# Mixture-of-experts decoder layer: expert loop over 64 experts, overflow rows in units of 32 through a second loop

## The chip, the cores and the metric

One core of one Trainium2 chip. The metric is the device time of one launch of the whole layer in microseconds (us), median of several runs. Beside it stands one profiled execution with its own span, from its first to its last instruction.

## The reference

One layer for 1104 tokens (16 meta tokens, a prompt of 1024, 8 samples of 8 tokens): latent attention and a gated linear recurrence side by side, a merge, a layer norm, and then the part that this change touches, a mixture of experts:

```python
scores = sigmoid(x @ router_w)                       # x: (N, 1024), 64 experts
_, idx = top_k(scores + router_bias, 8)              # 8 experts for each token
gate = scores[idx] / sum(scores[idx]) * 2.5
y[token] += gate * (silu(x @ w_gate[e]) * (x @ w_up[e])) @ w_down[e]   # 1024 -> 256 -> 1024, all e in idx
out = layer_norm(ALPHA * x + y + shared_expert(x))
```

All arrays are float32. The tokens choose their experts by data: 1104 x 8 = 8832 rows over 64 experts, 138 on average. Evaluating the routing of the reference on its own inputs gives more than 160 rows for 5 experts (162, 166, 168, 171 and 183 rows), and no expert has more than 192.

## The kernel before, in words

The layer runs in stages, each a block in which the five engines run their own programs and wait on semaphores. The last three matter here.

**`stage_route`** (L1895) computes the first layer norm, the router scores and the shared expert. For each (token, expert) pair it writes an entry (token number, factor) to a slot of a table in DRAM (`slot_table`, scattered by GpSimd at L1990). The slot is `place * 64 + expert`, where `place` is the row's position among the rows of its expert. Then VectorE counts on how many experts lie above 160 rows: `over` (L2256 to L2259), five chained steps for further multiples of 160, a running sum `ob`, and from it a list of blocks (`cols`, turned by TensorE at L2109 into `blocks_i`) and the number of pairs of blocks (`pairs_i`). SyncE (SP) loads the table back to SBUF (L1977, L1979) as `ent_main` (rows 0 to 127 of each block) and `ent_rest` (rows 128 to 159, four times below each other), for all seven layers of 160 rows. The main output rows `y` of shared expert and residual go to DRAM as `y_rows`.

**`stage_experts`** (L2339) is a loop over pairs of blocks. A block is 160 slots of one expert: 128 rows of `xg` ("main") and 32 rows of `xg_rest` ("rest"). Blocks 0 to 63 are the first 160 rows of the 64 experts, and further blocks hold what an expert has above 160 rows, again as full blocks of 160 slots whose empty slots carry an index out of range, which the indirect transfers skip. An odd number of blocks is filled up with an empty one. The two blocks of a pair use the buffers s = 0 (`mla` in the profile for gate and up) and s = 1 (`mix`).

For each block SP loads 3 x 1 MB of weights (`weights`, L2396): gate and up once the rest products of the same buffer are done (`rest_full`), down once the copy of the previous block's output is done (`part_copied`). GpSimd (POOL) copies the indices (`pick`), gathers the rows from `x_rows` (`gather`, L2435) and adds the results to `y_rows` by an indirect accumulating transfer (`scatter`, L2452), main and rest each; before the next scatter it waits until the last one has landed (`y_out`, seen as a wait of L2426). TensorE turns the rows (`turn` L2498, `turn_rest` L2503), multiplies the main rows in three products of split weights (high part, low part, `PRODUCTS`, L2529 and L2550) and the rest rows with the unsplit weights (L2519 and L2563). ScalarE makes the high parts (`round_weights`, L2601), VectorE the low parts (`part_weights`, L2676). The engines work on different blocks at once: while block n is multiplied down, block n + 1 goes through gate and up and block n + 2 is turned.

Which expert a block belongs to and which layer of the table it reads is data, so SP reads registers from SBUF at the head of each pair (`expert`, L2394, three loads) and POOL too (`layer`, L2422, five loads). Each engine reads the number of pairs at its start (L2365).

**`stage_out`** (L2750) loads `y_rows` back, when the last scatter has landed and the block has been closed, and computes the second layer norm.

## Time and profile before

| | |
|---|---|
| runs (median of 3) | 2381.16 us (2374.51 to 2383.53) |
| the profiled execution's own time | 2375.11 us |
| its span | 2373.3 us |
| TensorE / VectorE / ScalarE / GpSimd busy | 2167.6 / 1413.6 / 1092.8 / 872.3 us |
| mean granted TensorE clock | 0.957 of full |
| stage of the experts | about 1345 to 2328 us of the span |
| blocks of 160 slots | 70 (140 scatters of L2452, two for each) |

Busy time counts an engine's instructions. The share of DMA is the mean busy share of the core's 16 DMA engines. Idle time before an instruction is put down to what ended it.
### The profile page before, as it was taken

The numbers are of one execution on the slowest core, as the hardware profiler recorded it, in microseconds if no ns is written. First come the engines' busy times: TensorE is split into PE (matmuls) and PEld (weight loads), VectorE is DVE, ScalarE is ACT, GpSimd is POOL, SyncE is SP. The second block draws the span as 40 slices with busy tenths as digits, with TensorE's granted clock in tenths as the row PEclk, the third lists the DMA queues.
The fourth block names the chain that finished last, engine by engine and source line by source line (L and its number), as shares of the span: only waits on it lengthen the run. The fifth ranks groups of instructions, "written<-read, shape, count | busy, mean of one in ns | idle before, by whom it ended". The sixth has DMA issues, their size and how long they took to land. (4 is left out here: it accounts for less than half of the span.)

```text
span 2373.3 us, 47274 instructions
## 1 busy us (share of the span) xinstructions
PE 2167.6 (91%) x17792; PEld 1695.0 (71%) x17792; DVE 1413.6 (60%) x2572; ACT 1092.8 (46%) x1700; POOL 872.3 (37%) x957
## 2 busy tenths in 40 slices
PE   7999899899867799999999899999999999999990
PEld 7666667679856799996555477777777777777760
DVE  4667455422186545544672467777777777777765
ACT  3355433322143333331220266676666666676652
POOL 0112311000142000000343257767776767677763
PEclk9999899899978899999999999999999999999995
DMA  4000333311000555441042489999999999999944
GB/s 154 14 1 1 135 118 134 103 54 45 31 25 2 192 176 177 148 131 60 28 153 96 156 280 319 303 309 323 304 298 318 313 308 327 302 310 314 290 148 169
DMA packets 104577, 419.42 MB, mean 177 GB/s; under 512 B 26278, under 2 KB 37606, under 8 KB 74502
## 3 DMA queue, kind: packets, MB, share of 16 engines
q1 hardware_dynamic: 64038, 320.69, 37.9%
q0 software_dynamic: 40144, 96.21, 15.7%
q8 instruction: 74, 1.21, 0.2%
q10 hardware_dynamic: 288, 1.05, 0.1%
q14 instruction: 33, 0.27, 0.0%
HBM read 374.69 MB, written 63.09 MB: 184 GB/s over the span
## 5 line engine op out<-in xcount | busy, mean ns | idle before, releaser
L2676 DVE TENSOR_TENSOR split<-mix,split 128x2048 fp32r<-128x2048 f32 x140 | 320.1, 2287 | 241.2 <-ACT split L2601 203.1
L2452 POOL DMA_INDIRECT y_rows<-mix x140 | 363.5, 2596 | 117.2 <-issue 86.9
L2529 PE MATMUL banks<-split 128*128 128x512 f32 x1680 | 402.7, 395 | 0.3 <-DVE split L2676 0.3
L2529 PEld LDWEIGHTS banks<-split 128*128 128x128 f32 x1680 | 310.4, 188 | 77.0 <-issue 14.4
L2601 ACT CAST split<-mix 128x2048 fp32r<-128x2048 f32 x140 | 266.9, 1908 | 0.0
L1990 POOL DMA_INDIRECT slot_table<-route x72 | 69.5, 966 | 465.8 <-DVE route L2228 446.2
L2550 PE MATMUL banks<-split 128*128 128x512 f32 x840 | 211.4, 401 | 4.7 <-DVE split L2705 4.7
L1777 PE MATMUL banks<-merge_split 128*128 128x368 f32 x1152 | 201.6, 332 | 4.5 <-DVE merge_split L1842 4.5
L1777 PEld LDWEIGHTS banks<-merge_split 128*128 128x128 f32 x1152 | 195.5, 190 | 5.1 <-DVE merge_split L1842 5.0
L2435 POOL DMA_INDIRECT hq<-x_rows,mix x136 | 149.7, 1100 | 82.9 <-POOL mix L2427 60.1
L2550 PEld LDWEIGHTS banks<-split 128*128 128x128 f32 x840 | 153.8, 190 | 34.9 <-issue 4.8
L2676 DVE TENSOR_TENSOR split<-mla,split 128x2048 fp32r<-128x2048 f32 x70 | 159.6, 2280 | 7.5 <-ACT split L2601 7.5
L2426 POOL COPY mix<-mix 128x2 int32 x138 | 111.9, 811 | 123.1 <-DMA y_rows<-mix 99.8
L2623 ACT COPY mix<-banks 128x512 f32<-128x512 f32 x140 | 82.3, 588 | 116.0 <-PE banks L2550 115.2
L2601 ACT CAST split<-mla 128x2048 fp32r<-128x2048 f32 x70 | 134.1, 1916 | 0.0
L1764 PE MATMUL banks<-merge_split 128*128 128x368 f32 x576 | 105.7, 334 | 8.2 <-DVE merge_split L1842 4.6
L1828 ACT ACTIVATE merge_rest<-banks 128x368 f32<-128x368 f32 x48 | 23.0, 478 | 189.6 <-PE banks L1777 189.6
L1109 PE MATMUL banks<-inputs_split 128*128 128x512 f32 (+1 forms) x432 | 103.5, 401 | 5.7 <-DVE inputs_split L1183 5.6
L1764 PEld LDWEIGHTS banks<-merge_split 128*128 128x128 f32 x576 | 98.8, 191 | 9.0 <-DVE merge_split L1846 4.8
L1109 PEld LDWEIGHTS banks<-inputs_split 128*128 128x128 f32 (+1 forms) x432 | 80.6, 187 | 28.4 <-DVE inputs_split L1183 7.5
L2498 PE MATMUL banks<-base,hq 128*128 128x128 f32 x560 | 85.2, 275 | 14.0 <-DMA hq<-x_rows,mix 9.7
L1125 PE MATMUL banks<-inputs_split 128*128 128x368 f32 x576 | 96.8, 330 | 0.0
(401 smaller groups left out, 4023.5 us busy)
## 6 DMA issues: line engine op xcount, KB each, us to landing
mix<-in_w_exp_down SPq DMA_DIRECT2D x70, 1024.0 KB
mla<-in_w_exp_gate SPq DMA_DIRECT2D x35, 1024.0 KB
mla<-in_w_exp_up SPq DMA_DIRECT2D x35, 1024.0 KB
mix<-in_w_exp_gate SPq DMA_DIRECT2D x35, 1024.0 KB
mix<-in_w_exp_up SPq DMA_DIRECT2D x35, 1024.0 KB
raw<-in_w_merge SPq DMA_DIRECT2D x32, 768.0 KB
merge_rest<-in_w_merge SPq DMA_DIRECT2D x15, 768.0 KB
raw<-in_w_cols SPq DMA_DIRECT2D x11, 512.0 KB, 4.6
```

The source lines that it names most:

```text
L1109: ins = pe.matmul(PS[0:rows(i), 4 + u % 4], x[a][:, k, 128 * i:128 * i + rows(i)], w[:, p % 4, b, 512 * (k % 2):512 * (k % 2 + 1)], start= ...
L1125: ins = pe.matmul(bank3(g)[:, n], cols[:, a, k], x[b][:, k, CH * n:CH * (n + 1)], start=(k == 0 and j == 0), stop=(k == KD - 1 and j == 2))
L1764: ins = pe.matmul(branch_bank(u), w[u % WR][:, a, GATE + 128 * k:GATE + 128 * (k + 1)], b[:, e, c, k], start=(k == 0 and t == 0), stop=(k ...
L1777: ins = pe.matmul(gate_bank(u), w[u % WR][:, a, 128 * k:128 * (k + 1)], x[:, c, k], start=(k == 0 and t == 0), stop=(k == KD - 1 and t == 2))
L2426: pool.tensor_copy(dst[:, s, 0:2].bitcast(I32), ent_main[:, bass.ds(at, 1)].rearrange("p a w -> p (a w)").bitcast(I32)).then_inc(sem, 1)
L2435: pool.indirect_dma_start(out=dst[:, s], out_offset=None, in_=src, in_offset=bass.IndirectOffsetOnAxis(ap=gi[:, s, 2 * hf:2 * hf + 1].bitc ...
L2452: pool.indirect_dma_start(out=dst, in_=src[:, s], in_offset=None, compute_op=ALU.add, out_offset=bass.IndirectOffsetOnAxis(ap=si[:, s, 2 * ...
L2498: ins = pe.transpose(PS[:, XBANK[r], 128 * j:128 * (j + 1)], xg[:, s, 128 * k:128 * (k + 1)], S.ident)
L2529: ins = pe.matmul(PS[:, MBANK].rearrange("p (j n) -> p j n", j=2), xr[:, a, k], wr[:, s, GATE:UP + 1, b, DEXP * k:DEXP * (k + 1)], start=( ...
L2550: ins = pe.matmul(PS[:, DBANK[c]], hr[:, a, f], wdr[:, b, at:at + 512], start=(f == 0 and j == 0), stop=(f == 1 and j == 2))
L2601: act.copy(parts(s, j)[:, HI], raw[s][j]).then_inc(rounded[j], 1)
L2676: dve.tensor_tensor(parts(s, j)[:, LO], raw[s][j], parts(s, j)[:, HI].bitcast(F32), ALU.subtract).then_inc(parted[j], 1)
```

## The change

The loop of pairs runs over the 64 experts alone, with constant bounds: 31 passes and a last pair that is written out. SP and POOL no longer load registers in it, since expert and entry number follow from the loop counter. The rows that an expert has above 160 are cut into units of 32 (`MINIS`, at most 256), and a second loop over pairs of units, of at least one pass, stands behind the first on every engine. A unit uses the unsplit weights alone, as the rest rows do.

In `stage_route` the chain over `over` has 29 steps in place of 5 (`LAYERS` = 30), the columns of the list are worked out for two times 128 units, TensorE turns four columns in place of two, and only the first 160 rows of each expert are loaded back from the table.

In the second loop SP reads expert e and layer j of a unit from SBUF, waits for a free entry buffer (`mini_free`), loads the 32 entries four times, and then 3 x 1 MB of weights. POOL raises `mini_free` by two only once the last scatter of block 63 has landed, and by one after each unit's scatter has landed. POOL gathers the rows of both units of a pair, then scatters the first, waits for it to land, scatters the second, and waits again.

```diff
-VCAP = -(-T // CAP) * CAP
-KOVER = VCAP // CAP - 1
-SLOTS = EXPERTS * VCAP
-LAYERS = VCAP // CAP
+LAYERS = -(-(T - CAP) // REST)
+SLOTS = EXPERTS * (CAP + REST * (LAYERS + 1))
+MINIS = 256
...
-        for k in range(1, KOVER):
-            own.link(dve.scalar_tensor_tensor(over[:, k], PS[:, 6, 0:EXPERTS], float(CAP * (k + 1)), over[:, k - 1], ALU.is_gt, ALU.add))
+        for k in range(1, LAYERS):
+            own.link(dve.scalar_tensor_tensor(over[:, k % 2], PS[:, 6, 0:EXPERTS], float(CAP + REST * k), over[:, (k - 1) % 2], ALU.is_gt, ALU.add))
...
+        for z in range(2):
+            m = pid[:, z:z + 1]
+            (seven small steps that give expert and layer of 128 units)
...
     @block.sync
-        last = last_pair(sp)
-        with sp.Fori(0, last) as it:
-            e = [expert(2 * it + 1 + s) for s in range(3)]
+        with sp.Fori(0, LASTP) as it:
             for s in range(2):
                 n = 2 * it + s
                 sp.wait_ge(rest_full, n + 1)
-                weights(s, GATE, e[s + 1])
-                weights(s, UP, e[s + 1])
+                weights(s, GATE, n + 2)
+                weights(s, UP, n + 2)
                 sp.wait_ge(part_copied, 3 * n + 3)
-                weights(1 - s, DOWN, e[s])
+                weights(1 - s, DOWN, n + 1)
+        pairs = mini_pairs(sp)
+        with sp.Fori(0, pairs) as it:
+            for s in range(2):
+                m = 2 * it + s
+                e = sp.value_load(X.blocks_i[0:1, 0, bass.ds(m, 1)], min_val=0, max_val=EXPERTS - 1)
+                j = sp.value_load(X.blocks_i[0:1, 1, bass.ds(m, 1)], min_val=0, max_val=LAYERS)
+                sp.wait_ge(mini_free, m + 1)
+                for q in range(4):
+                    src = overflow[bass.ds(j, 1), bass.ds(e, 1)].rearrange("j e r w -> (j e r) w")
+                    sp.dma_start(ent_mini[REST * q:REST * (q + 1), s].bitcast(I32), src).then_inc(mini_in[s], 16)
+                sp.wait_ge(rest_full, EXPERTS - 1 + m)
+                weights(s, GATE, e)
+                weights(s, UP, e)
+                sp.wait_ge(mini_copied, m + 1)
+                weights(s, DOWN, e)
...
     @block.gpsimd
-            at = [layer(2 * it + j) for j in range(2 + (2 if not ends else 0) + (gathers == 2))]
+        pool.wait_ge(y_out[1], 32 * (LASTP + 1))
+        pool.sem_inc(mini_free, 2)
+        with pool.Fori(0, pairs) as it:
+            for s in range(2):
+                pool.wait_ge(mini_index, 4 * (2 * it + s) + 4)
+                pool.wait_ge(xrest_full, EXPERTS - 1 + 2 * it + s)
+                (gather of xg_rest[:, s]).then_inc(mini_x[s], 16)
+            for s in range(2):
+                pool.wait_ge(mini_copied, 2 * it + s + 3)
+                (scatter of y_rest[:, s]).then_inc(mini_out[s], 16)
+                pool.wait_ge(mini_out[s], 16 * (it + 1))
+                pool.sem_inc(mini_free, 1)
...
     @block.tensor
+        def mini(s, it):
+            m = 2 * it + s
+            pe.wait_ge(mini_x[s], 16 * (it + 1))
+            pe.wait_ge(mini_copied, m + 2)
+            turn_rest(s, None)
+            pe.wait_ge(xrest_copied, EXPERTS + 1 + m)
+            for j in (GATE, UP):
+                pe.wait_ge(raw_in[j][s], 16 * (EXPERTS // 2 + it + 1))
+            rest_products(s)
+            pe.wait_ge(h_made, 2 * EXPERTS + 1 + m)
+            pe.transpose(PS[:, HBANK, 2 * MAIN:3 * MAIN], h_rest, S.ident).then_inc(hT_full, 1)
+            pe.wait_ge(hr_parted, EXPERTS + 1 + m)
+            pe.wait_ge(raw_in[DOWN][s], 16 * (EXPERTS // 2 + it + 1))
+            down_rest_products(s).then_inc(mini_full, 1)
...
     @block.scalar
+                act.wait_ge(rest_full, EXPERTS + 1 + m)
+                gate_rest()
+                act.wait_ge(mini_free, m + 1)
+                act.wait_ge(mini_full, m + 1)
+                act.copy(y_rest[:, s], PS[:, EBANK, 0:256]).then_inc(mini_copied, 1)
...
     @block.vector
+        with dve.Fori(0, pairs) as it:
+            for s in range(2):
+                dve.wait_ge(mini_in[s], 64 * (it + 1))
+                (four steps that turn the 32 entries into indices of quarter rows; mini_index + 1 each)
+            for s in range(2):
+                (copy of the turned rows, product with the sigmoid, product with factor and up, copy of hT_rest)
```

The lines in parentheses stand for several lines of code. `rest_products` and `down_rest_products` are the loops of L2515 to L2520 and L2560 to L2564 under names of their own, and `gate_rest` is L2609 and L2610.

## Rows read from the trace of the kernel before

**Rows 1.** Stretches of the expert loop: width, busy of each engine, PEclk, DMA share, GB/s.
```profile
1400.00:2227.00 827.00, 806.90 (x7785) 619.40 (x7783) 609.29 (x728) 556.03 (x725) 575.71 (x605) 1.00 0.97 312
2213.00:2290.00 77.00, 76.14 (x751) 59.16 (x748) 57.10 (x67) 53.58 (x69) 58.03 (x60) 1.00 0.76 247
```
**Rows 2.** The page, part 5: all scatters of the expert loop.
```profile
L2452 POOL DMA_INDIRECT y_rows<-mix x140 | 363.5, 2596 | 117.2 <-issue 86.9
```
**Rows 3.** Timeline of SP's queue: issues of the down weights, one for each block.
```profile
1379.66 0.33 SPq L2399 DMA_DIRECT2D mix<-in_w_exp_down  x1
...
2213.77 0.33 SPq L2399 DMA_DIRECT2D mix<-in_w_exp_down  x1
...
2281.22 13.45 SPq L2399 DMA_DIRECT2D mix<-in_w_exp_down  x2
```
**Rows 4.** What TensorE waited for, 1379 to 2295 us: total, times, longest.
```profile
PE banks L2498 <- DMA hq<-x_rows,mix: 9.7, 11, 1.6
```
**Rows 5.** Timeline of the loop's first block, TensorE just resumed: start, duration.
```profile
1345.67 0.63 PE L2503 MATMUL banks<-base,hq 128*128 128x128 f32 x2
...
1349.29 0.42 DVE L2684 COPY mix<-banks 128x256 f32<-128x256 f32 x1
...
1349.77 3.16 PE L2519 MATMUL banks<-mla,mix 128*32 128x128 f32 x64 [2.61 <-DVE mix L2684]
...
1352.98 0.27 ACT L2609 ACTIVATE mix<-banks 64x128 f32<-64x128 f32 x1 [3.16 <-PE banks L2519]
...
1353.95 0.34 DVE L2693 SCALAR_TENSOR_TENSOR mix<-mix 64x128 f32<-64x128 f32 x1
```
**Rows 6.** Timeline of the loop's end.
```profile
2281.26 1.95 PE L2519 MATMUL banks<-mla,mix 128*32 128x128 f32 x64
...
2313.53 0.19 POOL L2426 COPY mix<-mix 128x2 int32 x1 [1.43 <-DMA y_rows<-mix]
...
2315.91 1.07 PE L2563 MATMUL banks<-mix 128*32 128x256 f32 x16
...
2317.05 0.37 ACT L2628 COPY mix<-banks 128x256 f32<-128x256 f32 x1 [0.44 <-PE banks L2563]
2318.26 1.56 POOL L2452 DMA_INDIRECT y_rows<-mix  x1 [4.43 <-ACT mix L2628]
```
**Rows 7.** Stretches around TensorE's pauses, columns as in the first group.
```profile
1349.00:1351.00 2.00, 1.24 (x24) 1.16 (x28) 2.00 (x5) 0.82 (x1) 1.13 (x3) 0.50 0.03 8
1353.00:1356.00 3.00, 2.75 (x12) 2.30 (x13) 1.37 (x4) 2.99 (x4) 0.98 (x1) 1.00 0.46 171
2312.00:2314.00 2.00, 2.00 (x6) 1.63 (x5) 0.00 (x0) 0.00 (x0) 0.41 (x3) 0.50 0.04 1
```
**Rows 8.** The page, part 6: one small transfer, median us from issue to landing.
```profile
out<-out SPq DMA_DIRECT2D x1, 64.0 KB, 2.1
```
**Rows 9.** A stretch in which little but weights is loaded, in the stage before.
```profile
1246.00:1250.00 4.00, 3.54 (x38) 2.80 (x38) 2.69 (x21) 0.43 (x1) 3.09 (x4) 1.00 1.00 410
```
**Rows 10.** Timeline: a gather inside the loop and TensorE's wait for it.
```profile
1597.79 1.04 POOL L2435 DMA_INDIRECT hq<-x_rows,mix  x1 [0.30 <-issue]
...
1606.90 0.65 PE L2498 MATMUL banks<-base,hq 128*128 128x128 f32 x4 [1.38 <-DMA hq<-x_rows,mix]
```
**Rows 11.** Transfers that write or read `y_rows`: us from issue to landing.
```profile
DMA to landing us min/median/max: 2.6/4.1/12.7
```
**Rows 12.** Register loads by line: min/median/max ns, first and last start us.
```profile
L2422 POOLq TENSOR_LOAD <-base x5: 287/290/292, 1616.1 to 1618.6; - x5
```
**Rows 13.** Timeline of the list of blocks in the stage before.
```profile
1281.94 1.26 DVE L2258 SCALAR_TENSOR_TENSOR route<-banks,route 128x64 f32<-128x64 f32 x5
...
1284.99 0.15 DVE L2270 TENSOR_SCALAR route<-route 128x1 f32<-128x1 f32 x1
...
1292.78 0.38 PE L2109 MATMUL banks<-base,route 128*1 128x128 f32 x2
```
**Rows 14.** DMA queues, 1400 to 2290 us: packets of the instruction queue, MB, share.
```profile
q14 instruction: 1, 0.01, 0.0%
```

More of the change, by code:

```diff
@@ L2466, in body @@
                     pool.sem_inc(passed, 1)
-                    gather(*ahead(s, it, 3), at[s + 3])
-                scatter(s, it, at[s], first)
+                    gather(*ahead(s, it, 3), n + 3)
+                scatter(s, it, n, first)
         for j in range(3):
```

203 lines of the change are left out of this document (118 added, 85 removed).

## The prediction

> **What bounds the kernel now.** I read three views, in this order. The stretches of the expert loop come first [rows 1]: in 827 us TensorE is busy for 806.9 at the full clock, and the 16 DMA engines are busy for 97% at 312 GB/s, so the loop sits at two limits at once. In the stretch that holds the blocks above 64, whose indirect transfers move almost nothing, the DMA share falls to 0.76 and TensorE stays at 99%. Second, the timeline of SP's queue gives the period [rows 3]. There is one down issue for each block. From 1379.66 to 2213.77 they are 61 blocks, 13.67 us each. The last one starts at 2294.33 (2281.22 + 13.45 - 0.34), six blocks after 2213.77: 80.6 us, 13.4 each. So a block costs 13.4 us on TensorE alone and 0.3 more when the transfers are full. Third, the waits: of TensorE's 20.1 us of idle time in those 827 us, the only large transfer wait is for gathered rows, 9.7 us in 11 waits over the whole loop [rows 4].
>
> There are 140 scatters, two for each block, so 70 blocks ran [rows 2]: 64 experts, the 5 blocks above 160 rows that the reference's routing gives, and one empty block to make pairs. All five experts stay at or under 192 rows, so the new loop gets 5 units and one empty one, three passes. What is bought for six blocks is six units.
>
> **Removed: six blocks.** 80.6 us [rows 3]. They are taken out of a saturated loop, so this counts in full.
>
> **Added: a chain that nothing covers.** The second loop starts on POOL's word, once the last scatter of block 63 has landed. SP stands at `mini_free` before it, and behind that wait stand the entries and all the unit's weights, so nothing is prefetched during the last blocks. I price one unit, from its rows landed to its output copied (C): two turns 0.63, copy 0.42, rest products 3.16, two steps on ScalarE at 0.27 and two on VectorE at 0.34, one turn of h at half of 0.63, a copy of 0.22 (half of 0.42), 16 down products, an output copy of 0.37 [rows 5, 6]. TensorE's clock decides. The figures of rows 5 were taken at 1.2 GHz, the level granted after a pause [rows 7]; at 2.4 GHz the same 64 products take 1.95 and the 16 take 1.07 [rows 6]. I scale 1.07 by 3.16 / 1.95 to 1.7 for 1.2 GHz, and the turns by the same ratio down for 2.4. With eight handovers of about 0.07 (1352.93 to 1352.98, 2316.98 to 2317.05) [rows 5, 6], C is 8.6 at 1.2 GHz and 6.4 at 2.4 GHz.
>
> After C comes the scatter (D): 0.84 from ScalarE's copy to its start, 1.56 for itself, 1.43 until the next instruction of POOL is let go [rows 6], 3.9 with a little for rows that are not skipped. Before C comes the gather (G): the same 0.84, 1.04 for itself [rows 10], and a landing that the trace does not show alone. Its bounds are 1.43, the landing of an almost empty scatter [rows 6], and 8.07, from the end of a gather at 1598.83 to TensorE at 1606.90 under full DMA load [rows 10]. The small stored transfer takes 2.1 [rows 8]. The DMA engines are mostly free in the second loop, so I take 2.0, and G is 3.9.
>
> The order of the programs makes a pass serial. POOL gathers for the next pair only when this pair's second scatter has landed, and TensorE turns the second unit only when the first one is copied. The first scatter runs beside the second unit's chain and costs nothing (3.9 under a chain of 6.4 or more). The next pair's first weights are asked for when that first scatter lands, and they need 3.15 MB / 410 GB/s = 7.7 us plus 2.1 [rows 8, 9]; they hide under the rest of the second unit, the scatter and the gather. VectorE makes the indices of both units before it copies the first one's rows: SP's four issues (0.33 each and a little between them, 0.45), a landing of 2.1 and four steps of 0.15 [rows 3, 8, 13] end about 4.5 us after the second scatter landed, as G and the turn do (3.9 + 0.63). I add 0.5 for the tie. A later pass is thus 3.9 + 0.5 + 2C + 3.9.
>
> The first pass starts with its entries: 1.9 of issues, 2.1 to land, 0.6 for indices, G, about 8.5 us. But the second unit's entries stand in SP's queue behind the first unit's 3 MB, so VectorE's copy may wait until about 12.6 (2.8 of issues + 2.1 + 7.7). The bounds are 8.5 plus a turn and 12.6, and I take the later. The Trainium skill, "DMA: Bandwidth & Descriptors", section "Queues, rings and completion order", says that one queue's descriptors are consumed in ring order on each DMA engine; no row here shows it, and by the opposite the sum would be 3.5 us smaller.
>
> With all at 1.2 GHz the first pass is 12.6 + 8.0 + 8.6 + 3.9 = 33.1 (the first turn lies inside 12.6) and a later one 25.5: 84.1 in all. With all at 2.4 GHz it is 12.6 + 6.0 + 6.4 + 3.9 = 28.9 and 21.1: 71.1. Which level holds? TensorE idles for more than 7 us before each first unit (D and G), and after a pause at the loop's end it stood at 0.50 at 2312; after it resumed at 1349.77 the clock was back at 1.00 in the stretch from 1353 [rows 7]. So the first unit of a pass runs at 1.2 GHz, and the second one probably in part at 2.4. I give the second one the middle, 1.1 less each: 84.1 - 3.3 = **80.8 us**.
>
> **Changed in the loop.** POOL's five register loads for each pair lie between two scatters and the next gather, five at 0.29 with the steps between them, 1616.1 to 1618.9 [rows 12]. Without them some gathers go out up to about 1 us sooner. The most that can be won is the 9.7 us of rows 4, and nothing if the DMA engines, at 97%, only serve the same bytes in another order. I take 3. SP's three loads lie ahead of a wait for the rest products and cost nothing now; POOL's wait for the landing of a scatter comes later than they did, too. The last scatter before the second loop is now of a real block: the median landing of all is 4.1 from issue against 1.56 + 1.43 [rows 6, 11], **+1.1**. The engines' load of the number of pairs moves from the head of the stage, where all wait for it, to behind the loop, where it hides under the last scatter: -0.7, two and a half times a load of 0.29 [rows 12].
>
> **Changed in the stage before.** Five chained steps take 1.26 us, so 24 more take 6.05, and the second half of the columns some 1.4 (scan and columns together took the 1.9 from 1283.20 to 1285.14). The list was ready at 1285.14 and is now at about 1292.6; TensorE comes for it at 1292.78, after its shared products [rows 13]. So it is covered by a hair, and each microsecond above that would show in full. TensorE turns four columns and not two: +0.4. The smaller table load ends under the same shared products and wins nothing.
>
> **The sum.** -80.6 + 80.8 + 1.1 - 0.7 + 0.4 - 3.0 = -2.0. The profiled execution took 2375.1 by its own time (span 2373.3), the median of the runs is 2381.2, 6.1 more. I forecast 2373.1 for a profiled run and **2379 us** for the median. By half a percent, 11.9 us, a measurement of this kernel can tell a change from none.
>
> **Rivals.**
> *The clock holds and the loop speeds up.* TensorE stays at 2.4 GHz through the second loop, and the earlier gathers win the whole 9.7: -80.6 + 71.1 + 1.1 - 0.7 + 0.4 - 9.7 = -18.4, 2363 us. For it: bursts of a pass follow each other closely, 1.00 came back within about 3 us [rows 7]. Against: the pause between passes, and 97% DMA share. Chance 0.20.
>
> *Slower: the unit's indirect transfers stand behind weights.* While the gather goes out, 3 MB of weights may still be moving, and then it lands after 8.07 as in rows 10, not 2.0. The first pass has its copy at 8.5 + 6.1 instead of 12.6, 2.0 more; each later one costs 6.1 more, so the second loop takes 95.0 and the sum is +12.2: 2393 us. It decides when a later pass loses about 6 us. With all at 1.2 GHz and no gain in the loop as well, it comes to 2400. For it: weights and rows share the engines. Against: by my times the weights have landed when the later gathers start. Chance 0.14.
>
> *The jumps cost.* Each engine jumps back twice in the second loop, and the instructions may have to be fetched again on the path. By the nearest row, a transfer's 2.1 us [rows 8] for each of the entry and two jumps, this is +6: 2385 us. The first loop argues against it: over 30 jumps of every engine in 890 us, and the instruction queue moved one packet [rows 14]. The Trainium skill, "Runtime: NRT & Kernel Launch", section "Instruction fetch mechanics", says that a taken branch to outside the window of instructions held forces a fetch before execution goes on; the trace bears this out only in so far as these loops seem to fit. Chance 0.08.
>
> *It doesn't do what it says.* An expert above 192 rows would bring a unit more, two of them a pass more, +25 us. The routing gives none, and 70 blocks agree. I give it no share.
>
> **How the numbers follow.** The likeliest case has 0.58, its own range 2370 to 2391. The range for all reaches from the first rival's 2363 to 2398, between the second rival's 2393 and the 2400 that it gives with the other costs at their upper ends. Faster by over 0.5% (under 2369.3): 0.20, the first rival. Slower (over 2393.1): 0.14, the second. Within: 0.66.
>
> **What the profile after would show.** The down issues should stop after 64 blocks with the period near 13.6, and 128 large-loop scatters. The second loop should last 71 to 95 us from the last landing, its first pass longer than the two others by 7 to 8. TensorE should be busy for under half of it, DMA in bursts near 400 GB/s, the clock between 0.5 and 1. L2109's four turns should still start at about 1292.8. I would be wrong if gathers or entries landed much later than 2.1 us, if the weights of a unit were on the path, or if the first loop's period moved by more than 0.15 us, since that is multiplied by 62.

## The result, and the profile after

The changed kernel takes 2390.76 us (median of 7 runs, 2385.66 to 2395.09), the kernel before 2380.02 us on the same chip (7 runs). The ratio is 1.0061, 95% interval 1.0043 to 1.008: slower by 0.6%, or 10.7 us, where I had forecast 2379 and no change that can be told. The time lies in my range, but the sign is that of a case to which I had given 0.14. The profiled execution has a span of 2388.9 us; that of before had 2373.3.

The page of the changed kernel, tenths of 40 equal slices of the span (59.7 us each):

```profile
PE   8999899899877799999999799999999999999430
...
PEclk9999899899978899999999999999999999999755
DMA  4000423311100655431141489999999999999554
```

The two slices before the last show what is new: TensorE falls from nine tenths to four and three at a clock of 0.7 and 0.5, while the DMA engines are half idle. Most of these two slices is the second loop. First the part that answers to [rows 1] and [rows 3], the windows of the first loop (length, then busy us of each engine with its instructions, granted clock, DMA share, GB/s) and the end of SP's queue in it (start, length, what was issued):

```profile
1400.00:2190.00 790.00, 776.71 (x7497) 596.64 (x7490) 583.99 (x697) 535.89 (x698) 559.95 (x581) 1.00 0.97 314
```

```profile
1384.74 0.33 SPq L2403 DMA_DIRECT2D mix<-in_w_exp_down  x1
...
2212.90 0.34 SPq L2403 DMA_DIRECT2D mix<-in_w_exp_down  x1
```

From block 2 to block 63 it is (2212.90 - 1384.74) / 61 = 13.58 us a block, against 13.67 in [rows 3]: 5.9 us less over the loop. TensorE's wait for gathered rows is 3.8 us in 7 waits, against 9.7 in 11 [rows 4].

Now the second loop, the timeline from the last main scatter (L2465) on. L2428 loads a unit's entries, L2817 makes indices of them, L2403 loads its weights, L2500 gathers, L2531 turns the rows, L2539 and L2589 are the products, L2736 copies the output, L2506 scatters; in brackets is the idle time ahead and what ended it:

```profile
2238.24 1.55 POOL L2465 DMA_INDIRECT y_rows<-mix  x1 [0.30 <-issue]
2243.02 1.74 SPq L2428 DMA_DIRECT2D mix<-slot_table  x4
...
2248.01 1.79 SPq L2428 DMA_DIRECT2D mix<-slot_table  x4
...
2253.79 0.69 PE L2531 MATMUL banks<-base,hq 128*128 128x128 f32 x2 [18.71 <-DMA hq<-x_rows,mix]
2255.96 0.67 DVE L2817 TENSOR_SCALAR mix<-mix 32x1 int32<-32x1 int32 x4 [9.38 <-DMA mix<-slot_table]
...
2265.11 1.64 POOL L2506 DMA_INDIRECT y_rows<-mix  x1 [6.49 <-ACT mix L2736]
...
2269.88 1.73 SPq L2428 DMA_DIRECT2D mix<-slot_table  x4
2270.67 0.37 ACT L2736 COPY mix<-banks 128x256 f32<-128x256 f32 x1 [2.59 <-PE banks L2589]
2271.86 0.35 SPq L2403 DMA_DIRECT2D mla<-in_w_exp_gate  x1
2271.91 1.57 POOL L2506 DMA_INDIRECT y_rows<-mix  x1 [5.16 <-ACT mix L2736]
2272.30 0.38 SPq L2403 DMA_DIRECT2D mla<-in_w_exp_up  x1
...
2281.19 1.72 SPq L2428 DMA_DIRECT2D mix<-slot_table  x4
2282.27 1.07 POOL L2500 DMA_INDIRECT hq<-x_rows,mix  x1 [8.79 <-issue]
...
2286.18 3.83 PE L2539 MATMUL banks<-mla,mix 128*32 128x128 f32 x64 [0.70 <-DVE mix L2821]
...
2292.15 1.94 PE L2589 MATMUL banks<-mix 128*32 128x256 f32 x16 [0.32 <-DVE mix L2827]
...
2303.69 0.37 ACT L2736 COPY mix<-banks 128x256 f32<-128x256 f32 x1 [3.60 <-PE banks L2589]
...
2311.86 1.72 SPq L2428 DMA_DIRECT2D mix<-slot_table  x4
...
2335.79 1.58 POOL L2506 DMA_INDIRECT y_rows<-mix  x1 [7.84 <-ACT mix L2736]
```

From the end of the last main scatter (2239.79) to the end of the last unit's (2337.37) it is **97.6 us**, where my terms make 81.9 (80.8, and 1.1 for the landing of the real block). This stretch is what I call the length of the second loop. The rows from 2271.91 on show the largest part. The second unit's scatter ends at 2273.48, and SP is let go by its landing only at 2281.19, 7.7 us later; POOL stands idle for 8.79 us before its next gather. As that scatter began, SP asked for 3 MB of weights for the next pass (from 2271.86 on). The windows of that landing, of the second pass's, and of the three passes:

```profile
2273.50:2281.20 7.70, 0.00 (x0) 0.00 (x0) 0.00 (x0) 0.00 (x0) 0.00 (x0) 0.52 0.97 391
2304.90:2311.80 6.90, 0.00 (x0) 0.00 (x0) 0.00 (x0) 0.00 (x0) 1.58 (x1) 0.50 0.84 320
```

```profile
2243.00:2281.20 38.20, 9.21 (x166) 6.39 (x166) 4.29 (x20) 1.81 (x6) 5.33 (x4) 0.68 0.66 250
2281.20:2311.90 30.70, 13.67 (x166) 8.45 (x166) 3.71 (x16) 1.81 (x6) 5.32 (x4) 0.50 0.57 214
2311.90:2338.00 26.10, 12.51 (x166) 8.15 (x166) 3.12 (x12) 1.81 (x6) 5.32 (x4) 0.57 0.33 123
```

While the scatter lands, no engine works and the transfers run at 391 GB/s: those are the weights, 3.15 MB in about 8 us. The first two passes take 38.2 and 30.7 us, where I had 33.1 and 25.5 for the low clock. And the clock was low for both units of the second pass, not for the first alone.

The first theory after the result was therefore: contention of each pass's last scatter with the next pass's weights costs 10 of the 15.7 us that were missed, the low clock 4 to 5. The rivals: the clock alone; the jumps; the loop's first start.

### The profile page after: what moved, and what is told of

Read it like the earlier page. It is cut to its first block and busy times, and to the rows that moved or that the text cites. A ratio compares the mean times of both kernels' runs of the same rounds, so it can differ in the third digit from the quotient of the medians.

```text
span 2388.9 us, 45337 instructions
## 1 busy us (share of the span) xinstructions
PE 2125.3 (89%) x17518; PEld 1659.3 (69%) x17518; DVE 1370.1 (57%) x2580; ACT 1043.0 (44%) x1648; POOL 832.3 (35%) x908
## 5 line engine op out<-in xcount | busy, mean ns | idle before, releaser
L2743 DVE TENSOR_TENSOR split<-mix,split 128x2048 fp32r<-128x2048 f32 x128 | 292.6, 2287 | 220.2 <-ACT split L2655 188.6
L2465 POOL DMA_INDIRECT y_rows<-mix x128 | 333.2, 2603 | 101.3 <-issue 75.6
L2560 PE MATMUL banks<-split 128*128 128x512 f32 x1536 | 367.8, 395 | 0.0
L2560 PEld LDWEIGHTS banks<-split 128*128 128x128 f32 x1536 | 283.4, 188 | 69.9 <-issue 12.7
L2655 ACT CAST split<-mix 128x2048 fp32r<-128x2048 f32 x128 | 243.9, 1907 | 0.0
L2581 PE MATMUL banks<-split 128*128 128x512 f32 x768 | 193.2, 401 | 4.6 <-DVE split L2743 4.6
L2448 POOL DMA_INDIRECT hq<-x_rows,mix x124 | 137.7, 1110 | 75.4 <-POOL mix L2440 54.5
L2581 PEld LDWEIGHTS banks<-split 128*128 128x128 f32 x768 | 140.8, 190 | 32.1 <-DVE split L2743 4.8
L2439 POOL COPY mix<-mix 128x2 int32 (+1 forms) x126 | 113.2, 899 | 111.8 <-DMA y_rows<-mix 90.1
L2743 DVE TENSOR_TENSOR split<-mla,split 128x2048 fp32r<-128x2048 f32 x64 | 146.0, 2281 | 4.2 <-ACT split L2655 4.2
L2655 ACT CAST split<-mla 128x2048 fp32r<-128x2048 f32 x64 | 122.6, 1916 | 0.0
L1123 PE MATMUL banks<-inputs_split 128*128 128x368 f32 x576 | 96.8, 330 | 0.0
L1123 PEld LDWEIGHTS banks<-inputs_split 128*128 128x128 f32 x576 | 96.7, 188 | 0.1
```

What stands on the lines that cost most here:

```text
L1123: ins = pe.matmul(bank3(g)[:, n], cols[:, a, k], x[b][:, k, CH * n:CH * (n + 1)], start=(k == 0 and j == 0), stop=(k == KD - 1 and j == 2))
L2439: pool.tensor_copy(dst[:, s, 0:2].bitcast(I32), ent_main[:, bass.ds(at, 1)].rearrange("p a w -> p (a w)").bitcast(I32)).then_inc(sem, 1)
L2448: pool.indirect_dma_start(out=dst[:, s], out_offset=None, in_=src, in_offset=bass.IndirectOffsetOnAxis(ap=gi[:, s, 2 * hf:2 * hf + 1].bitc ...
L2465: pool.indirect_dma_start(out=dst, in_=src[:, s], in_offset=None, compute_op=ALU.add, out_offset=bass.IndirectOffsetOnAxis(ap=si[:, s, 2 * ...
L2560: ins = pe.matmul(PS[:, MBANK].rearrange("p (j n) -> p j n", j=2), xr[:, a, k], wr[:, s, GATE:UP + 1, b, DEXP * k:DEXP * (k + 1)], start=( ...
L2581: ins = pe.matmul(PS[:, DBANK[c]], hr[:, a, f], wdr[:, b, at:at + 512], start=(f == 0 and j == 0), stop=(f == 1 and j == 2))
```

## The experiments

The runs of this part were made in three groups, each on one chip of its own, each with the kernel before beside them: the first four kernels with it at 2359.93 us, the unaltered kernel, register loads, early start and interleaved order at 2362.63, the 64 fillers and the last kernel at 2360.16. Between groups I compare each kernel's distance to the kernel before, and stretches within traces.

### No second loop

```diff
-        pairs = mini_pairs(...)
-        with ...Fori(0, pairs) as it:      # on all five engines
-            ...
```

> The changed kernel without its second loop on any engine; POOL still waits for the last scatter of block 63. It leaves out the rows above 160 of five experts. The changed kernel's trace has 97.6 us from the end of block 63's last scatter (2239.8) to the end of the last unit's scatter (2337.4). If the second loop is what made the kernel slower than forecast, this one takes 95 to 98 us less than the changed kernel (2390.8), 2293 to 2296. If instead the earlier stages or the first loop got slower by the change, the difference stays what I had forecast for the loop, about 82 us, and this kernel takes about 2309.

Measured: 2279.47 us (one run), span 2277.7, 80.5 below the kernel before. The expected 2293 to 2296 was worked out at the first comparison's level, where the kernel before takes 20 us more, so only the distance can be used. The unaltered changed kernel was run in the next group and stands 18.4 above it, so its second loop costs about 98.9 us. The same number tests all the rest of my sum: without the added loop it says -80.6 + 1.1 - 0.7 + 0.4 - 3.0 = -82.8, and -80.5 was measured. Everything but the 80.8 came out right together, within 2.3. That is closer than one run can show, since the ten runs of the kernel before in this group lie from 2355.91 to 2366.26, and it tests the sum and none of its terms.

### Weights of 64 columns in place of 2048

```diff
+        def thin(s, j, e):
+            sp.dma_start(raw[s][j][:, 0:64], src[:, 0:64]).then_inc(raw_in[j][s], 16)
...
-                weights(s, GATE, e)
+                thin(s, GATE, e)          # the same for UP and DOWN
```

> The changed kernel, where the second loop loads only 64 of 2048 columns of each weight block of a unit, with all semaphores and orders as they are. It leaves out most of the weights of the units, so their rows are wrong. Theory A, the second scatter of a pass lands late (7.6 and 5.3 us after its issue ends, against 3.1 and 1.8 for the first scatter) because it shares the DMA engines with the 3 MB that the first scatter's landing let go: then both land within 2 to 3 us, and the first pass starts its copy at about 9 us instead of 13.7 after the second loop's first entry load. Second loop 97.6 - 8 - 4.5 = about 85 us. Theory B, a scatter of 128 quarter rows with an accumulate simply takes that long behind a second scatter, whatever else moves: the landings stay at 5 to 8 us, and only the first pass is shorter, about 93.

Measured: 2366.91 us (one run). From the last main scatter's end to the last unit's scatter's end it is 81.3 us (2232.24 to 2313.55). The ends of its first two passes, and the windows of its three:

```profile
2261.79 1.57 POOL L2511 DMA_INDIRECT y_rows<-mix  x1 [6.38 <-ACT mix L2741]
...
2265.78 1.73 SPq L2433 DMA_DIRECT2D mix<-slot_table  x4
...
2285.22 1.58 POOL L2511 DMA_INDIRECT y_rows<-mix  x1 [4.89 <-ACT mix L2741]
...
2289.24 1.72 SPq L2433 DMA_DIRECT2D mix<-slot_table  x4
```

```profile
2235.40:2265.80 30.40, 12.01 (x166) 7.80 (x166) 4.28 (x20) 1.81 (x6) 5.32 (x4) 0.61 0.09 16
2265.80:2289.30 23.50, 9.30 (x166) 6.48 (x166) 3.70 (x16) 1.81 (x6) 5.31 (x4) 0.72 0.10 17
2289.30:2314.00 24.70, 12.36 (x166) 8.15 (x166) 3.13 (x12) 1.81 (x6) 5.31 (x4) 0.57 0.04 7
```

The scatter now lands 2.4 us after its end, twice (2263.36 to 2265.78, 2286.80 to 2289.24), where it took 7.7 and 5.3 beside the weights. So what the weights' transfers cost is real, and the theory that the scatters are slow by themselves (93 us expected) is out. The clock stayed low too (0.61, 0.72, 0.57, against 0.68, 0.50, 0.57 in the changed kernel), but not everywhere: the second unit of the second pass ran at the full clock (6.5 us from scatter to scatter). Added up, the six chains are 49.8 us here and 51.7 in the changed kernel, so 2.0 of the 16.3 us that the loop is shorter are the clock's, and the clock alone cannot be what was missed. The later passes, 23.5 and 24.7, now lie between my 21.1 and 25.5: a later pass with its weights gone takes what I had predicted with them. (The whole, 81.3 against my 81.9, agrees more closely than it should: my first pass had the wait of the entries behind weights in it, which is gone here.)

### Weights asked for first

```diff
         with sp.Fori(0, pairs) as it:
             for s in range(2):
-                (entries of unit s, weights of unit s)
+                unit_weights(s, 2 * it + s)
+            for s in range(2):
+                unit_entries(s, 2 * it + s)
```

> The changed kernel with one order turned round on SP: in a pass the weights of both units are asked for first (gate and up once the rest products of the buffer are done, down once the last output is copied), then the entries of both, which wait for their buffer. Same bytes, same products. Theory A: the first pass no longer waits for entries behind 3 MB (copy at 9 us, not 13.7), and gate and up of the next pass have landed before the second scatter; only 1 MB of down still meets it. Second loop 97.6 - 4.5 - 6 = about 87, the kernel about 2380, 0.5% faster than the changed one, close to the kernel before. Theory B (scatters slow by themselves): 93, the kernel 2386.

Measured: 2373.64 us (7 runs, 2365.49 to 2383.41), ratio to before 1.0067 [1.0043, 1.0091], 13.7 us above it where the unaltered changed kernel stands 18.4 above. The second loop takes 88.0 us. The first pass gained most: 17.9 us from the first entries to the first scatter, against 22.5 in the unaltered kernel's run of the next group. The later passes gained little, 30.2 and 28.5 us from first scatter to first scatter against 30.6 and 30.7. SP's queue shows why:

```profile
2254.27 0.33 SPq L2403 DMA_DIRECT2D mix<-in_w_exp_down  x1
2255.11 1.57 POOL L2514 DMA_INDIRECT y_rows<-mix  x1 [6.24 <-ACT mix L2744]
2256.10 8.66 SPq L2435 DMA_DIRECT2D mix<-slot_table  x8
...
2265.42 1.07 POOL L2508 DMA_INDIRECT hq<-x_rows,mix  x1 [8.74 <-DVE mix L2825]
```

Both units' weights are now asked for from 2242 to 2254, while the units are still at work, and the small transfers behind them are late in the same way, with the DMA engines at a share of 0.98 or more until 2260: eight entry loads take 8.66 us where the first eight of the loop took 4.95, and POOL waits 8.74 us for the indices. The wait changed its name, not its length. That the whole came near the expected 87 is partly luck: against the unaltered kernel's 98.1 us the first pass gives 4.6, the later passes together 2.5 where 6 were expected, and 3.0 come from the last unit, which ran at the full clock (6.5 us from scatter to scatter against 9.5).

### Filler products ahead of each pass, 40 and 64

```diff
         def mini(s, it):
+            if s == 0:
+                for _ in range(40):       # 64 in the second kernel
+                    pe.matmul(PS[:, MBANK]..., xr[:, HI, 0], wr[:, 0, GATE:UP + 1, HI, 0:DEXP], start=True, stop=True)
             pe.wait_ge(mini_x[s], 16 * (it + 1))
```

> The changed kernel with 40 more products of 128x512 into an unused bank on TensorE ahead of each pass's wait for gathered rows, about 10 us of work in time in which TensorE idles. In the changed kernel a unit's chain from its turn to its output's copy takes 9.8 and 9.5 us in the second pass, all at a granted clock of 0.50, and 6.8 for the second unit of the first pass, at 1.00. Theory clock: all chains fall to about 6.8, the second loop to 97.6 - 3 - 5.7 - 4.5 = about 84 us. If the chain's length is in the handovers and not in the clock, it stays within 2 us of 97.6. If the added products run past the landing of the rows, the passes get longer by that.

Measured with 40: 2369.86 us (one run), but the second loop took 96.8 us, not 84. Its windows around the second pass, three microseconds each (the clock is third from the end, then DMA share and GB/s):

```profile
2257.00:2260.00 3.00, 3.00 (x15) 2.49 (x14) 0.00 (x0) 0.00 (x0) 0.00 (x0) 1.00 0.99 388
2260.00:2263.00 3.00, 0.78 (x4) 0.32 (x2) 0.00 (x0) 0.00 (x0) 0.10 (x1) 1.00 0.09 26
2263.00:2266.00 3.00, 0.00 (x0) 0.00 (x0) 0.58 (x4) 0.00 (x0) 0.97 (x1) 0.84 0.36 72
2266.00:2269.00 3.00, 1.92 (x26) 1.55 (x30) 0.42 (x1) 0.00 (x0) 1.03 (x1) 0.50 1.03 431
```

The clock is full while the filler runs, and back at 0.50 when the unit's own products start at 2266.4. So 40 were too few to test the price. The run stands 9.9 us above the kernel before, where the unaltered kernel stands 18.4 above. Its second loop gives only 1.3 of the difference, and 3.2 lie ahead of it (the last main scatter ends at 2219.39, in the unaltered kernel's profile on another chip at 2222.57); one run does not tell more.

> The changed kernel with 64 filler products, not 40, ahead of each pass of units; their sums are never read. 40 of them took 9.0 us and ended 5.6 us before the second pass's rows landed; the granted clock was 1.00 while they ran and 0.50 again when the unit's own products began, and the second loop took 96.8 us against 98.1 in the unaltered kernel on this chip. 64 should take 14.8 us and end as the rows land (14.9 us after the previous chain's end). If the low clock costs what the prediction took (2.2 us a unit) or the 2.6 that chains of 9.5 and 6.8 us differ by, the four units of passes two and three give back 9 to 10: a second loop of 87 to 89 and a kernel of about 2371 where the unaltered one takes 2381. If only loads, gathers and landings matter there, since the products wait for them anyway, it stays at 95 to 98 and 2378 to 2383. If the filler itself outlasts the landing, the loop becomes longer.

Measured with 64: 2376.96 us (7 runs), ratio 1.0067 [1.0043, 1.0091] to before, second loop 95.0 us. In the second pass the clock now held through both units, in the third pass through the first unit, and the loop still gained only 3 us. The timeline of the second pass:

```profile
2277.00 1.96 PE L2539 MATMUL banks<-mla,mix 128*32 128x128 f32 x64 [0.70 <-DVE mix L2825]
...
2283.52 1.96 PE L2539 MATMUL banks<-mix 128*32 128x128 f32 x64 [0.51 <-DVE mix L2825]
...
2286.83 1.73 SPq L2428 DMA_DIRECT2D mix<-slot_table  x4
...
2289.91 1.58 POOL L2506 DMA_INDIRECT y_rows<-mix  x1 [4.89 <-ACT mix L2740]
...
2298.77 1.73 SPq L2428 DMA_DIRECT2D mix<-slot_table  x4
```

The 64 rest products take 1.96 us in both units, and scatter follows scatter by 6.5 us, where the unaltered kernel has 9.5. But the scatter, issued 3 us sooner, lands 7.3 us after its end (2291.49 to 2298.77), and not 5.4. From SP's entries for the next first unit to the second unit's landing it is 11.9 us here, 12.7 and 12.9 in the unaltered kernel, 11.3 and 13.0 in the profile of the first comparison, 7.2 and 7.0 with thin weights. So the weights' transfer sets this stretch, whatever the clock does; the second unit's chain lies beside it. The kernel with register loads (below) agrees: its second units took 7.9 us from scatter to scatter where the unaltered kernel's took 9.5, and its steps from first scatter to first scatter were 30.8 and 30.5 us all the same. Of a pass with a successor only the first unit's chain is on the path. Its gain shows in the third pass, 27.7 us from scatter to scatter against 30.7. In the second it was lost again: its 64 fillers began at the low clock, took 16.4 us and ran to 2276.1, 1.6 us past the time at which 14.8 would have ended. My expectation of 9 to 10 us counted four chains, where one in each pass and the very last count.

### The changed kernel once more

> The changed kernel itself, unaltered, on the chip on which the others of this group run. If the first comparison's ratio of 1.0061 holds, it takes 2374 us here (1.0061 x 2359.9), bounds 2370 to 2379, and the kernel with no unit (2279.5) and the one with thin weights (2366.9) stand 95 and 7 below it, the latter near the 12 that the theory of contended scatters expects and far from the 0 to 4 that the theory of a low clock alone expects. If the slowing was a matter of the chip, it takes 2360. The time from the last main scatter's end to the last unit's scatter's end should again be 97 to 98 us, against 96.8 with filler products and 88.0 with weights first.

Measured: 2381.01 us (6 runs, 2374.70 to 2385.69), ratio 1.0085 [1.0059, 1.0111], 18.4 us above the kernel before. That is above the 2370 to 2379 that I expected from the first ratio; the two intervals overlap, so the slowing is not a matter of one chip. It measured 10.7 us on one and 18.4 on the other. The second loop takes 98.1 us (2222.57 to 2320.62). The second units' chains were slow in all three passes here, 9.5 us from scatter to scatter. The theory's size follows from this trace and that with thin weights, 98.1 against 81.3 us. Of the 16.7 us between them 3.9 are chains (53.7 against 49.8), that is, the clock, which was higher in the thin run. The other 12.8 are the weights' transfers: 5.1 for the first copy, where the entries stand behind weights (13.7 us after the first request against 8.6; I had priced 12.6 - 8.5 = 4.1), 6.9 for the two waits from a copied output to the next pass's first request (8.8 and 7.8 against 4.9 and 4.9), which I had not priced, and 0.8 for the gathers. Against the first profile of the changed kernel the same sum is 2.0 for chains and 14.3 for transfers. The two traces are one execution each on two chips. The second loops of the three profiles in the changed order, without fillers and with their weights, are 96.4 (the kernel with register loads), 97.6 and 98.1 us.

### GpSimd's register loads put back

```diff
         def body(it, gathers, ends, first=False):
+            for j in range(5):
+                pool.value_load(X.blocks_i[0:1, 1, bass.ds(2 * it + j, 1)], min_val=0, max_val=LAYERS)
```

> Changes one thing in the changed kernel: GpSimd reads five registers per pair of blocks again in the first loop, as before the change. The theory that these reads held up GpSimd's gathers, and through them TensorE, expects the changed kernel's first loop to become longer by about what it had gained, 0.09 us a block or 5.9 us over 61 blocks (bounds 3 to 8), and TensorE's wait for gathers in the loop to rise by about as much. The rival, that the weights' transfers set the loop's pace (their share was 0.97 before and after) and the 5.9 us were a difference of two executions, expects no change beyond 2 us.

Measured: 2381.25 us (5 runs), the unaltered kernel's 2381.01. Block 2 to block 63 takes 833.0 us. In the seven profiles of kernels whose first loop is the changed one the stretch takes 826.8 to 837.5, mean 830.2, and 834.1 in the kernel before. So a gain of the size that I took, 3 us, can be neither shown nor excluded; the 5.9 us of the first pair of profiles are within the spread. TensorE's wait for gathers was 27.4 us in the unaltered kernel on this chip, 31.6 with the loads, 30.8 in the interleaved kernel below, which has none, and 29.2 in the kernel without units: it does not tell the two apart either.

### The first pass started early, and then an interleaved order

```diff
+        for s in range(2):
+            unit_entries(s, s, wait=False)    # SP, ahead of the first loop
...
         body(LASTP - 1, 1, False)
+        unit_gathers(0)                       # POOL, ahead of the last pair
         body(LASTP, 0, True)
```

The later passes ask for weights ahead of entries, as in the kernel with weights asked for first, so the edit changes two things in the unaltered kernel.

> The changed kernel with weights asked for ahead of entries, as in the kernel with weights first, and with the first pass's entries loaded at the start of the stage and its two gathers issued ahead of the last pair of blocks; nothing is left out. In the changed kernel 22 us lay between the first entries' load and the first unit's scatter, where the unit's own chain is 6.8. If that is all waiting for loads and gathers, the first unit's chain can start when TensorE is done with the last block, and its scatter follows the last main scatter at once: 20 to 22 us less, and 2 less from the weights' order in the later passes, so about 2350 here if the changed kernel takes 2374, and 10 under the kernel before. The rival, that something else is late in the first pass (the landing of the last main scatters, then the weights of the first units), expects no more than 10 us less: 2364.

Measured: 2362.65 us (12 runs, eleven from 2357.93 to 2369.63 and one of 3121.60), ratio 0.9999 [0.9981, 1.0017]: 18.4 less than the changed kernel, and even with the one before. The second loop is 80.8 us, but that alone overstates the gain: from block 63's down request to the end of the last main scatter it is 31.5 us here and 27.5 in the unaltered kernel. I expected 22 in the first pass, 2350 in all; the rival, that something else is late there, such as the landing of the last main scatter, expected 2364 and has the reason. TensorE did finish the first unit at once, but ScalarE could not copy its result:

```profile
2233.52 1.55 POOL L2478 DMA_INDIRECT y_rows<-mix  x1 [0.30 <-issue]
...
2242.30 0.37 ACT L2757 COPY mix<-banks 128x256 f32<-128x256 f32 x1 [11.64 <-POOLq L2527]
```

It waits for POOL's word that the last main scatter has landed, which took until 2242.3 beside the first units' weights, 7.2 us after its end.

```diff
-            (gathers of both units; scatter, wait, scatter, wait)
+            unit_gather(0, it)
+            landed(1, it - 1)
+            unit_gather(1, it)
+            unit_scatter(0, it)
+            landed(0, it)
+            unit_scatter(1, it)
```

> As the kernel with the early start, and in the later passes the next first unit's gather is issued before the wait for the second unit's scatter, and the requests stand in the order weights of the first unit, entries of the first, entries of the second, weights of the second. Nothing is left out. With weights first alone, a pass still took 28.5 to 30.3 us, because the entries' loads then stood beside 6 MB of weights (8.7 us from request to the last of eight issued, against 3.9) where the scatter had stood before. If the contention only moves from one small transfer to the next unless it is laid under a unit's chain, this order gives passes of about 26: 4 less in each of two, so 2342 to 2346 here. If the cost of a pass is the low clock and the chain of handovers instead, it gives no gain over the early start (within 2 us).

Measured: 2353.74 us (12 runs), ratio 0.9965 [0.9949, 0.9982], 8.9 under the early start alone (expected 8; the 2342 to 2346 in all missed, since they stood on the early start's 2350). The passes are 24.8 and 27.2 us (first scatters at 2240.29, 2265.13, 2292.28), expected 26.

### Entries of all units ahead, gathers two units ahead

```diff
+        with sp.Fori(1, pairs) as it:         # SP, ahead of block 63's down weights
+            for s in range(2):
+                unit_entries(s, 2 * it + s)   # each unit has its own place
...
+        with pool.Fori(1, pairs) as it:
+            for s in range(2):
+                unit_gather(s, 2 * it + s + 2)
+                landed(1 - s, it - 1 + s)
+                unit_scatter(s, 2 * it + s)
```

> The same units, with every unit's entries loaded before the last block of the first loop is done (each has its own place), and each unit's gather issued two units ahead, as soon as its buffer is free; weights are asked for when their buffers are free. Nothing is left out. No unit's chain then waits for a load of entries, a gather or the landing of another unit's scatter. If these waits are what the second loop's time is made of, six chains of 7 to 9.5 us stand end to end: the last unit's scatter ends 40 to 55 us after the last main scatter's end, against 98 in the changed kernel and 70 in the one with interleaved order, and the kernel takes 2325 to 2338. If the weights' transfers are the bound instead (3 MB a unit at 391 GB/s is 8.0 us, six of them 48, the first two asked for before the first loop ends), it comes out at the same 45 to 55, but the products wait for weights, not for rows. If the units are bound by the scatters' order (one has to land before the next starts, 4 us alone, up to 9 beside weights), six of them take up to 55 as well, and the chain of waits shows it. The rival, that the interleaved order already took what there was, expects no less than 2350.

Measured: **2335.87 us** (6 runs, 2329.03 to 2343.97), ratio to before 0.9899 [0.9869, 0.9929]. The second loop is 51.6 us (2228.87 to 2280.51), inside the expected 40 to 55. Its scatters:

```profile
2240.81 1.58 POOL L2515 DMA_INDIRECT y_rows<-mix  x1 [10.54 <-ACT mix L2770]
...
2249.01 1.58 POOL L2515 DMA_INDIRECT y_rows<-mix  x1 [5.23 <-DMA y_rows<-mix]
...
2255.21 1.58 POOL L2515 DMA_INDIRECT y_rows<-mix  x1 [3.24 <-DMA y_rows<-mix]
...
2261.33 1.58 POOL L2515 DMA_INDIRECT y_rows<-mix  x1 [3.16 <-ACT mix L2770]
...
2271.10 1.59 POOL L2515 DMA_INDIRECT y_rows<-mix  x1 [6.81 <-ACT mix L2770]
...
2278.92 1.59 POOL L2515 DMA_INDIRECT y_rows<-mix  x1 [4.85 <-ACT mix L2770]
```

The second and third wait for the landing of the scatter before them, the last three for their unit's output. No unit waits for a load of entries any more, and in the view of waits no product waits for weights. The first scatter starts 11.9 us after the last main one's end, which again landed beside the units' weights; in the windows DMA is at 1.00 from 2232 to 2243 and at 0.83 from there to 2265. All three explanations in the expectation gave 40 to 55 us, so the time does not choose among them: by the waits it is landings for the first three units and the units' own chains for the last three, with the DMA engines near their limit beside the first half. What each of the parts of this edit is worth was not measured. This is the version that beats both kernels, the one before by 24.3 us and the changed one, by the distances, by 42.7.

## Why the prediction was wrong

**The failed step is the landing in D,** "1.43 until the next instruction of POOL is let go", taken from an almost empty scatter with the queues idle [rows 6]. From copied output to the next pass's first request a second unit's D was 10.2 us in the first pass (2271.04 to 2281.19) and 7.8 in the second (2304.06 to 2311.86), where I had 3.9: +10.1 together. With thin weights the two were 4.9 and 4.9. So 8.2 of the 10.1 are the weights' transfer, and 1.9 were missing even without it (2.4 us from the scatter's end to the landing, not 1.43). My own text held both halves of the fact. It said that the next pair's weights are asked for when the first scatter lands, and that they "hide under the rest of the second unit, the scatter and the gather". I checked that the weights would be there in time. I did not check what they do to the small transfer that lies beside them. I called the DMA engines "mostly free in the second loop"; over each pass they were (0.66, 0.57 and 0.33), but not in the stretches in which a small transfer was under way (0.97 and 0.84). And [rows 11] had a landing of up to 12.7 us in it.

**The rival had the mechanism and the wrong place.** "The unit's indirect transfers stand behind weights" predicted +12.2 and 2393 us; the first comparison gave +10.7 and 2391, the one on another chip +18.4. It put the cost at the gather, and its argument against itself was right: in the later passes the rows were with TensorE 2.5 and 3.9 us after the gather began (2282.27 to 2284.80, 2312.92 to 2316.81). It was the scatter ahead of the gather that stood there. In the first pass the gather was late as well: from its start to TensorE it took 6.3 us (2247.54 to 2253.79), with thin weights 2.7. That was one of my signs of being wrong, but the wait for the second unit's entries covered it. My chance of 0.14 rested on one of three small transfers.

**C at 1.2 GHz was too short,** 8.6 where the second and third passes show 9.5 to 9.8 (and 8.6 once, where the clock came back in the middle). I took 3.16 us for 64 products from [rows 5]; they take 3.64 to 3.83. That block was not at the low clock throughout. The down products take 1.94, not 1.7. With the clock low for the second unit too, where I gave it the middle, the six chains were 51.7 us and not 47.7, +4.0. But the fillers and the kernel with register loads show that this term is not worth its face: in a pass with a successor the second unit's chain lies beside the weights' transfer, and what it loses by the clock the landing behind it gives back. So the +10.1 and the +4.0 are not two causes side by side, and a higher clock alone would not have saved all of the 4.0.

**The first pass was right in kind.** The second unit's entries stood behind the first unit's weights; the copy came 13.6 us after the first request, I had 12.6. The rule of the Trainium skill, "DMA: Bandwidth & Descriptors", section "Queues, rings and completion order", that one queue's descriptors are consumed in ring order, goes with this row: the entries, asked for from 2248.01, were with VectorE at 2255.96, about when the 3 MB asked for ahead of them were through (asked for from 2245.01, 7.5 us at the 418 GB/s of that stretch, an estimate). By the opposite they would have come 4.0 us sooner (1.79 + 2.1 after 2248.01), but the copy only 2.2, since the first unit's own rows were turned at 2254.48; so the 3.5 that I gave for it was too much. The rule speaks of one queue. The scatter goes through another (GpSimd's), and it was late just the same, so one queue's order is not what held it. Thin weights take the bytes from the shared DMA engines and from memory alike; which of the two held it is not shown.

**The shares of the miss add up.** From output to next request +10.1, chains +4.0, the first copy +1.0, the start of the loop +0.7 (block 63's scatter landed 3.2 us after its end, I had 2.5), gathers -0.2: 15.6, against 97.6 - 81.9 = 15.7.

**Removed blocks, loop gain and the rest** were right as a sum (-82.8 predicted, -80.5 measured without the second loop, one run). How much of it is the loop's gain stays open: its size lies within the spread of executions. The 9.7 us of the first rival did not show.

**The stage before** came out nearly as drawn, but the list was no longer ready in time. 29 steps took 7.46 us, as 5 took 1.26 [rows 13], and TensorE stood 0.54 us for the list at its four turns:

```profile
1287.44 7.46 DVE L2256 SCALAR_TENSOR_TENSOR route<-banks,route 128x64 f32<-128x64 f32 x29
...
1298.78 0.15 DVE L2268 TENSOR_SCALAR route<-route 128x1 f32<-128x1 f32 x1 [0.53 <-DVE route L2267]
...
1298.99 0.60 PE L2107 MATMUL banks<-base,route 128*1 128x128 f32 x4 [0.54 <-DVE route L2268]
```

It is about 0.8 us in all with the longer turns (0.60 against 0.38), where I had 0.4. The span's difference of 15.6 us holds another 4.7 that lie before the change: this execution was that much later when the merge's last weights were asked for (1066.5 against 1061.8).

**The jumps** did not cost what that rival said. The loop with thin weights has all of them, and its later passes lie inside my bounds. From 2240 to 2316 the instruction queue moved two packets (0.03 MB), with the weights and with thin ones.

## What to carry to other kernels

When work is taken out of a saturated loop into a short loop of its own, write down for each small transfer on its path which bulk transfer is asked for just before it. A scatter of 32 rows that must land before anything else may start took here about as long as the 3 MB beside it, and moving the request only gives the wait to the next small transfer. What helped, as one bundle, was to take the small transfers off the path: indices loaded before the loop, gathers two units ahead, and the wait for a scatter's landing moved to just before the next scatter. And measure whether a chain is on the path before paying for its speed: a faster second chain was worth nothing here in the passes that had a successor, since a landing beside 3 MB stood behind it.

## What the runs showed of the hardware

An accumulating scatter of 32 x 4 quarter rows landed 2.4 us after its end with quiet DMA engines (twice, with thin weights), and 5.3 to 7.7 us after it beside 3 MB of weights on another queue (window at 391 GB/s). Eight small loads that took 4.95 us to issue with quiet engines took 8.66 and 7.51 behind the rest of 6 MB of weights on their own queue (the last of them asked for 1.8 us earlier): there the issuing engine is held as well, not only the landing.

TensorE's clock was at 0.50 again by 2266, when its last filler product had ended at 2260.8, and after 64 fillers, which ran up to the unit, it stayed at 1.00 through both units of the second pass (1.96 us for the 64 products of each). In the third pass it fell for the second unit, whose 64 products took 3.50. In the unaltered kernel the level was not the same from one execution to the next: the first pass's second unit ran at 1.00 in the first profile (6.8 us from scatter to scatter) and at the low clock in the other (9.5). The two executions ran on two chips. A loop like this one has no one time, and a price for it needs both levels.
